# Experts of a two-block network: the gather and the return of tokens as single rounded products, weights of the slots beside the first expert, norms in one operation a block

## The reference, cut to what matters

```
hx2 = modulate(rmsnorm(x, norm2_g), mod_x[3], mod_x[4])     # x * rsqrt(mean x^2 + eps) * g * (1 + scale) + shift
probs = softmax(h @ router_w); sel = probs + router_b
best_group = argmax over 4 groups of the sum of the two best sel of its 4 experts
idx = the two best experts inside best_group; combine = their probs, normalised
for e in 16 experts: out += combine[:, e] * ((silu(h @ w_gate[e]) * (h @ w_up[e])) @ w_down[e])
x = x + mod_x[5] * out
return rmsnorm(x, final_norm_g)
```

## Time and profile before

| | |
|---|---|
| median of 3 runs | 1496.63 us (1496.12 to 1498.65) |
| the profiled execution | 1495.06 us |
| its span, first to last instruction | 1493.7 us |
| mean granted TensorE clock | 0.954 |
| PE busy | 1357.3 us (91%) |
| PEld busy | 1186.4 us (79%) |
| DVE busy | 1096.1 us (73%) |
| ACT busy | 751.1 us (50%) |
| HBM read | 309.49 MB |

### The profile page before, as it was taken

The page is one execution under the profiler, slowest core; times in us unless marked ns, Lnnn a source line. Parts: engine busy times, 40 slices in busy tenths (PEclk is TensorE's granted clock), DMA queues, the critical chain, the costliest instruction groups (busy, mean ns, idle before and its releaser), DMA issues.

```text
span 1493.7 us, 20983 instructions
## 1 busy us (share of the span) xinstructions
PE 1357.3 (91%) x7872; PEld 1186.4 (79%) x7872; DVE 1096.1 (73%) x1502; ACT 751.1 (50%) x956; POOL 0.4 (0%) x5
## 2 busy tenths in 40 slices
PE   6879799998999977999987899898699999999996
PEld 6778699997777766998986678898687787777884
DVE  5767678777697867686786757876566868788686
ACT  3432444453666674454433543443146757566563
POOL 0000000000000000000000000000000000000000
PEclk9969999999999988999999899999799999999999
DMA  8628686773677754756573252321075977878772
GB/s 332 231 104 312 196 309 247 279 277 144 214 277 268 262 190 155 289 208 215 184 252 115 92 183 71 100 71 40 1 239 174 349 250 274 279 240 325 240 258 104
DMA packets 84212, 311.90 MB, mean 209 GB/s; under 512 B 9488, under 2 KB 9712, under 8 KB 83504
## 3 DMA queue, kind: packets, MB, share of 16 engines
q1 hardware_dynamic: 82080, 298.88, 57.0%
q10 hardware_dynamic: 2032, 11.69, 2.4%
HBM read 309.49 MB, written 1.05 MB: 208 GB/s over the span
## 4 chain that ended last, share of the span: by engine, by line
PE 66%; DVE 22%; ACT 7%; DMA 3%; issue 2%; DVEq 0%; ACTq 0%; SPq 0%
PE ps L433 65%; DVE w_low L392 8%; DVE junk L392 4%; ACT w_high L392 3%; DMA ring<-stream 1%; DMA ring<-moe 1%; DVE t_one L392 1%; DVE r_two L392 1%; DVE rs L392 1%; DVE x L392 1%; ACT h_high L392 1%; DVE t_two L392 1%; PE ps L1032 1%; DVE y_experts L392 1%; DVE all L392 0%
## 5 line engine op out<-in xcount | busy, mean ns | idle before, releaser
L392 DVE TENSOR_TENSOR w_low<-ring,w_high 128x1024 fp32r<-128x1024 f32 x368 | 451.0, 1225 | 149.9 <-ACT w_high L392 120.0
L392 ACT ACTIVATE w_high<-ring 128x1024 fp32r<-128x1024 f32 x368 | 390.3, 1061 | 294.2 <-PE ps L433 173.6
L433 PE MATMUL ps<-x_high,w_high 128*128 128x256 f32 (+1 forms) x784 | 237.1, 302 | 34.4 <-DVE x_low L392 22.6
L433 PE MATMUL ps<-x_low,w_high 128*128 128x256 f32 (+1 forms) x784 | 233.9, 298 | 0.0
L433 PE MATMUL ps<-x_high,w_low 128*128 128x256 f32 (+1 forms) x784 | 233.7, 298 | 0.0
L433 PEld LDWEIGHTS ps<-x_high,w_high 128*128 128x128 f32 x784 | 155.5, 198 | 44.3 <-issue 16.1
L433 PEld LDWEIGHTS ps<-x_low,w_high 128*128 128x128 f32 x784 | 155.7, 199 | 2.5
L433 PEld LDWEIGHTS ps<-x_high,w_low 128*128 128x128 f32 x784 | 155.4, 198 | 2.8
L392 DVE CUSTOM_DVE_ANT_0 junk<-ring,cond 128x1024 f32<-128x1024 f32 x109 | 133.6, 1226 | 29.9 <-DMA ring<-stream 16.8
L433 PE MATMUL ps<-h_high,w_high 128*128 128x256 f32 x512 | 146.7, 287 | 6.6 <-DVE h_low L392 4.2
L433 PE MATMUL ps<-h_low,w_high 128*128 128x256 f32 x512 | 145.6, 284 | 0.0
(11 more groups left out here) (299 smaller groups left out, 2066.7 us busy)
## 6 DMA issues: line engine op xcount, KB each, us to landing
ring<-stream SPq DMA_DIRECT2D x376, 512.0 KB, 4.8
ring<-moe SPq DMA_DIRECT2D x192, 512.0 KB, 4.7
tab_two<-tab ACTq DMA_DIRECT2D x1, 2824.0 KB, 15.0
gw<-gw ACTq DMA_DIRECT2D x1, 2304.0 KB, 13.2
cond<-cvec ACTq DMA_DIRECT2D x3, 512.0 KB, 5.5
x<-xT ACTq DMA_DIRECT2D x1, 1024.0 KB, 11.7
ctx<-ctxT ACTq DMA_DIRECT2D x1, 1024.0 KB, 4.8
pos<-posT ACTq DMA_DIRECT2D x1, 1024.0 KB, 8.3
```

Source lines behind the costliest of these rows:

```text
L392: return op(*a, **k).then_inc(self.sem, 1)
L433: return pe.matmul(out, stationary, moving, start=start, stop=stop, skip_group_check=True)
```

## The change

- The tokens are held as a high and a low part. ACT writes the modulated T2 (bias added in ACT's Identity), so that DVE's norm is 8 operations on X with scale and root row in one. The transposes become plain products with the identity; after ACT's rounded copy (`XT[0]`) TensorE adds the product of minus identity and that copy to the same PSUM bank, and ACT copies what is left to `XT[1]`.
- ONEHOT and SCAT have type fp32r. Gather: a product of each part with ONEHOT into banks of its own, each one MATMUL instruction; ACT copies the high one, DVE the low one.
- The DIAG products go behind the first piece of gate(0), and the slots' weights behind gate(0).
- Results: ACT writes the rounded YS (two halves) or YES of group 0, DVE subtracts to get their low parts (`result_lows`), and the scatters are products of each part with SCAT. `summed` makes YES[0] after place 12, by two copies of 128x1024 once y_add is 10. The scatters wait for the low parts.
- The last norm is 8 operations with gain and root row in one.

The diff, cut to its core:

```diff
+Y_SUMS, Y_LOW = {4: 2, 8: 6, 12: 10}, {1: 4, 2: 8, 0: 12, 3: 14}
+XG_BANKS = ((4, 6), (5, 7), (2, 3), (4, 6))
...
tensor_program
-    pe.wait_ge(s.t2, 4 * MOD_MOE + 4)
-    for b in range(2):
-        for k in range(KT):
+    for k in range(KT):
+        if k % 2 == 0:
+            pe.wait_ge(s.x_high, x_splits(MOD_MOE) + k // 2 + 1)
+        for b in range(2):
             ins = mm(PS[:, 4 + b, 0:NE], m.T2[:, k, b * P:(b + 1) * P], m.par("rw", k * NE, NE), k == 0, k == KT - 1)
...
-            ins = pe.transpose(PS[:, 2 * b + k // 4, ...], m.T2[:, k, b * P:(b + 1) * P], m.ident)
+            ins = mm(PS[:, 2 * b + k // 4, ...], m.T2[:, k, b * P:(b + 1) * P], m.ident, k % 4 == 0, False)
+        ins.then_inc(s.xt_mm, 1)
+    for b in range(2):
+        pe.wait_ge(s.xt, b + 1)
+        for c in range(2):
+            ins = mm(PS[:, 2 * b + c, :], m.NEG, m.XT[0][:, b, c * 512:(c + 1) * 512], False, True)
...
+    def tokens(out, part, k, slots):
+        for b in range(2):
+            ins = mm(out, m.XT[part][:, b, k * P:(k + 1) * P], m.ONEHOT[:, b, slots], b == 0, b == 1)
+        return ins
+    pe.wait_ge(s.xt, 4)
     pe.wait_ge(s.onehot, 2)
+    for r in range(4):
+        if r == 3:
+            pe.wait_ge(s.xg_high, 1)
+            pe.wait_ge(s.xg_low, 1)
+        for part in range(2):
+            for j in range(2):
+                ins = tokens(PS[:, XG_BANKS[r][part], j * 256:(j + 1) * 256], part, 2 * r + j, slice(0, 256))
...
     def other_tokens():
         for k in range(KT):
+            pe.wait_ge(s.xg_high, 4 + max(k - 1, 0))
+            tokens(PS[:, 4 + k % 2, 0:CAP - 256], 0, k, slice(256, CAP)).then_inc(s.xg_mm, 1)
+            pe.wait_ge(s.xg_low, 4 + max(k - 1, 0))
+            tokens(PS[:, 6 + k % 2, 0:CAP - 256], 1, k, slice(256, CAP)).then_inc(s.xg_mm, 1)
...
     def scatter(i, r):
-        if i == 0:
-            pe.wait_ge(s.y_add, 6)
-        else:
-            pe.wait_ge(s.y_out, i + 2)
-            if i < 3:
-                pe.wait_ge(s.y_add, 2 * i)
+        pe.wait_ge(s.y_add, Y_LOW[i] - (i > 0 and r < 2))
...
-                mm(out, m.YE[:, 0, blk], m.SCAT[:, 0, :], True, False)
-                ins = mm(out, m.YE[:, 1, blk], m.SCAT[:, 1, :], False, True)
+                for n in range(4):
+                    ins = mm(out, m.YES[n % 2][:, n // 2, blk], m.SCAT[:, n // 2, :], n == 0, n == 3)
             else:
-                ins = mm(out, m.YS[:, blk], m.SCAT[:, i + 1, :], True, True)
+                for n in range(2):
+                    ins = mm(out, m.YS[n][:, blk], m.SCAT[:, i + 1, :], n == 0, n == 1)
...
scalar_program
+    for k in range(KT):
+        if k % 2 == 0:
+            act.wait_ge(s.t2, 4 * MOD_MOE + k // 2 + 1)
+        A(m.T2[:, k, :], m.T1[:, k, :], ACT.Identity, s.x_high if k % 2 else None, bias=m.MOD[:, 120 + k:121 + k])
...
     for p in range(NE):
         high_upto(w + 5)
+        if p > 0:
+            summed(p - 1)
         turned(p)
...
vector_program
-    rms_rows(9, m.X[:, :, :], m.T1[:, :, :])
-    modulate_norm(MOD_MOE, m.T1, "n2g", 120, 128)
+    op(vv.tensor_scalar, sc2, m.MOD[:, 128:136], 1.0, None, ALU.add)
+    op(vv.tensor_tensor, sc2, sc2, m.par("n2g", 0, 8), ALU.mult)
+    root(9)
+    for k in range(KT):
+        op(vv.scalar_tensor_tensor, m.T1[:, k, :], m.X[:, k, :], sc2[:, k:k + 1], m.RSTD, ALU.mult, ALU.mult, inc=...)
...
+    def result_lows(p):
+        i, j = EXPERTS[p]
+        if j == 3:
+            for c in range(2):
+                vv.wait_ge(s.y_out, {1: 4, 2: 6, 0: 8, 3: 10}[i] - 1 + c)
+                if i == 0:
+                    op(vv.tensor_tensor, m.YES[1][:, c, :], m.YE[:, c, :], m.YES[0][:, c, :].bitcast(F32), ALU.subtract, inc=s.y_add)
+                else:
+                    half = slice(c * 512, (c + 1) * 512)
+                    op(vv.tensor_tensor, m.YS[1][:, half], PS[:, 4 + c, :], m.YS[0][:, half].bitcast(F32), ALU.subtract, inc=s.y_add)
...
         low_upto(w + 4)
+        if p > 0:
+            result_lows(p - 1)
         if back is not None:
             results(back, 0)
...
-    rms_rows(10, m.X[:, :, :], m.T1[:, :, :])
+    root(10)
     for k in range(KT):
-        op(vv.tensor_scalar, m.X[:, k, :], m.T1[:, k, :], m.par("fing", k), None, ALU.mult, inc=s.final)
+        op(vv.scalar_tensor_tensor, m.X[:, k, :], m.X[:, k, :], m.par("fing", k), m.RSTD, ALU.mult, ALU.mult, inc=s.final)
```

More of the change, by code:

```diff
@@ L215, in __init__ @@
         self.KF = view("kf", aKF, 2048)
-        place(P)
+        self.NEG = rounded("neg_ident", place(P), P)
         aX, aXL = place(4096), place(4096)
@@ L314, in __init__ @@
         self.XGH, self.XGL = (rounded("xg_" + n, a, 8 * CAP).rearrange("p (k s) -> p k s", k=KT) for n, a in (("high", aX), ("low", aB)))
-        self.XT = view("x_tokens", aB + 5120, 2048).rearrange("p (b d) -> p b d", b=2)
-        self.ONEHOT = view("onehot", aB + 7168, 2 * CAP).rearrange("p (b s) -> p b s", b=2)
-        self.SCAT = view("scat", aB + 8448, 1280).rearrange("p (i t) -> p i t", i=5)
+        self.XT = tuple(rounded("x_tokens_" + n, a, 2048).rearrange("p (b d) -> p b d", b=2) for n, a in (("high", aB + 5120), ("low", aT1)))
+        self.ONEHOT = rounded("onehot", aB + 7168, 2 * CAP).rearrange("p (b s) -> p b s", b=2)
+        self.SCAT = rounded("scat", aB + 8448, 1280).rearrange("p (i t) -> p i t", i=5)
         self.ROUT = view("rout", aB + 9728, 1024)
@@ L323, in __init__ @@
         self.YE = view("y_experts", aKF, 2048).rearrange("p (a d) -> p a d", a=2)
-        self.YS = view("y_single", aT1 + 1024, 1024)
+        self.YES = tuple(rounded("y_experts_" + n, a, 2048).rearrange("p (a d) -> p a d", a=2) for n, a in (("high", aT2), ("low", aB + 5120)))
+        self.YS = tuple(rounded("y_single_" + n, a, 1024) for n, a in (("high", aT1 + 1024), ("low", aT1)))
     def place(self, n):
@@ L967, in tensor_program @@
     mm(PS[:, 6, 8:12], m.ONES, group_of(0), False, True).then_inc(s.cnt, 1)
-    pe.wait_ge(s.xt, 2)
-    pe.wait_ge(s.onehot, 2)
-    for k in range(KT):
-        for b in range(2):
-            ins = mm(PS[:, 4 + k // 2, (k % 2) * 256:(k % 2 + 1) * 256], m.XT[:, b, k * P:(k + 1) * P], m.ONEHOT[:, b, 0:256], b == 0, b == 1)
-        if k % 2:
-            ins.then_inc(s.xg_mm, 1)
-    pe.wait_ge(s.diag, 2)
-    for b in range(2):
-        ins = mm(PS[:, 2, b * P:(b + 1) * P], m.ONES, m.DIAG[:, b, :], True, True)
@@ L978, in tensor_program @@
-    ins.then_inc(s.db_mm, 1)
-    pe.wait_ge(s.comb_w, 1)
-    for i in range(5):
-        for b in range(2):
-            ins = mm(PS[:, 3, 4 * i:4 * i + 4], m.ONEHOT[:, b, i * P:(i + 1) * P], m.ROUT[:, 848 + 4 * b:852 + 4 * b], b == 0, b == 1)
-    ins.then_inc(s.cw_mm, 1)
+    def tokens(out, part, k, slots):
[3 more added lines that the diff above has]
+    pe.wait_ge(s.xt, 4)
+    pe.wait_ge(s.onehot, 2)
@@ L985, in other_tokens, with weights_of_slots @@
+    def weights_of_slots():
+        pe.wait_ge(s.comb_w, 1)
+        for i in range(5):
+            for b in range(2):
+                ins = mm(PS[:, 7, 4 * i:4 * i + 4], m.ONEHOT[:, b, i * P:(i + 1) * P].bitcast(F32), m.ROUT[:, 848 + 4 * b:852 + 4 * b], b == 0, b == 1)
+        ins.then_inc(s.cw_mm, 1)
     def other_tokens():
+        pe.wait_ge(s.scat, 5)
+        pe.wait_ge(s.cw, 1)
         for k in range(KT):
-            pe.wait_ge(s.xg_low, 4 if k < 4 else k + 1)
-            for b in range(2):
-                ins = mm(PS[:, 4 + k % 4, 0:CAP - 256], m.XT[:, b, k * P:(k + 1) * P], m.ONEHOT[:, b, 256:CAP], b == 0, b == 1)
@@ L1037, in down @@
         if j == 0 and i >= 2:
-            pe.wait_ge(s.y_out, i + 1)
+            pe.wait_ge(s.y_add, Y_LOW[i - 1])
         for n in range(4):
@@ L1479, in results, with summed @@
                 act.wait_ge(s.sc_mm, 4 * (i - 1))
-            A(m.YS, PS[:, 4:6, :].rearrange("p c n -> p (c n)"), ACT.Copy, s.y_out)
+            for c in range(2):
+                A(m.YS[0][:, c * 512:(c + 1) * 512], PS[:, 4 + c, :], ACT.Copy, s.y_out)
+    def summed(p):
+        if EXPERTS[p] == (0, 3):
+            act.wait_ge(s.y_add, Y_SUMS[p])
+            for a in range(2):
+                A(m.YES[0][:, a, :], m.YE[:, a, :], ACT.Copy, s.y_out)
     high_upto(W_MOE + 8)
@@ L2139, in vector_program, with first_low @@
         op(vv.tensor_scalar, m.DIAG[:, b, :], m.ident, dest[:, b:b + 1], None, ALU.mult, inc=s.diag)
+    def first_low(r):
+        vv.wait_ge(s.xg_mm, 2 * r + 2)
+        op(vv.tensor_copy, m.XGL[:, 2 * r:2 * r + 2, 0:256], PS[:, XG_BANKS[r][1], :].rearrange("p (k s) -> p k s", k=2), inc=s.xg_low)
+        low_upto(W_MOE + r + 1)
     first_max(ML, NE, EX, st[:, 34:36], TM)
     op(vv.scalar_tensor_tensor, ML, EX, -3e30, ML, ALU.mult, ALU.add)
+    for r in range(4):
+        first_low(r)
     first_max(ML, NE, E2, st[:, 36:38], TM)
```

52 lines of the change are left out of this document (33 added, 19 removed).

## The result

The changed kernel needs 1503.3 us (median of 6 runs, 1503.06 to 1504.44) beside 1496.72 us of the kernel before, measured with it. The ratio is 1.0039 with a 95% interval of 1.0026 to 1.0052, so it is slower by 0.26 to 0.52%. The profiled execution is 1503.29 us with a span of 1502.0.

What follows compares the result with a forecast made beforehand. TensorE bounds the experts, except where it stops. Front -0.8 - 3.3 - 1.35, group 1 +1.4 + 1.5, group 2 +0.8, group 0 +2.4 + 2.2, short stop +1.5, tail -1.7 make +2.65 us: 1497.7 profiled, 1499.3 median, range 1493.3 to 1504.

Steps and rivals of the forecast that it cites:

- Norm and router: From the MoE norm's reciprocal to the count: router ends 3.8 us sooner, transposes take most back, 0.8 us left.
- Gather: Gather of the tokens: 32 instructions in 5.7 us against 9.0 before, a gain of 3.3 us (2.0 to 5.0).
- Other slots: Other slots' products: 8.7 us against 10.0, with TensorE standing from +2.1 to +5.0; gain 1.35 us.
- one of two short stops: Half clock after the stops of 2.9 (other slots) and 2.4 us (group 2): one is paid, 1.5 us.
- Group 1: Return of group 1: TensorE stands 4.6 us; DVE's two extra operations cost +1.4 us, half clock 1.5 us.
- Group 2: Return of group 2: 2.4 us idle for the low part, less 1.6 given back by the products: +0.8 us.
- What follows is TensorE's: Behind group 2's return, with two tiles, TensorE sets the time; no size of its own.
- Group 0: Return of group 0: 5.8 us stop, less 4 x 0.93; taken as +2.4 us, plus 2.2 us of half clock.
- Tail: End of the kernel: new last norm -1.2 us, last square sums no longer queued -0.5; together -1.7 us.
- The clock holds: Rival: full clock through the new stops takes away 2.55 us, giving 1494.1 us; chance 0.18.
- The low parts come in time: Rival: the returns' 7.3 us are kept, 1482 us, believed only as far as 1489.6; chance 0.07.
- The slow rival: Rival: half clock for six us and more after every pause, +5.8 us on the sum, 1505 us; chance 0.17.

Runs made afterwards that it cites:

- norm_only: The kernel before with the new last norm and nothing else: 1495.04 us, ratio 0.9990.
- results_only: The kernel before with the split returns alone: 1510.64 us, ratio 1.0105.
- front_norm: The changed kernel with the plain returns put back: 1489.12 us, ratio 0.9954 of the kernel before.
- early_lows: The changed kernel with results' low parts made after gate(p+1)'s first low part, not its fourth, and ACT's group 0 copies two pieces earlier: 1493.86 us, ratio 0.9978.
- front_warm: front_norm with 14 unread products filling TensorE's stop among the other slots' products: 1487.36 us, ratio 0.9935.
- stops_warm: The changed kernel with unread products filling three stops (other slots, group 1, group 0): 1493.43 us, ratio 0.9983.
- warm_stop: The changed kernel with 24 unread products ahead of the wait of group 0's first scatter: 1500.19 us, ratio 1.0018.
- dve_extra: front_norm with unread DVE operations of like size added where the results' low parts would be made: 1493.8 us, ratio 0.9986.
- high_only: The changed kernel without the results' low parts: no subtraction, scatters of the high part alone: 1489.39 us, ratio 0.9961.

## Why the prediction was right or wrong

**Ahead of the change: not foreseen, +3.1 us.** The sum began at R9, with nothing ahead of it. R9 lies between 1056.89 and 1063.34 in the 14 profiles, and kernels alike up to there differ: norm_only and results_only, both of the old front, 1059.17 and 1056.89; front_norm and early_lows, both of the new one, 1060.06 and 1063.34. In the changed kernel two places are seen: the chain has a transfer of the stream of 5.28 us at 147.08 where the kernel before had 3.69 at 147.06, and 16 products at 155.73 that took 5.20 in place of 3.73 us, at half clock. All six runs of the changed kernel lie within 1.4 us, though. Nor is the slow form spread evenly over the 14 profiles: those 16 products took 3.72 us in the three kernels with the old front (before, results_only, norm_only) and in front_warm, and 5.1 to 6.7 us in the ten others, all with the new front; the mean of R9 is 1058.4 us with the old front and 1060.4 with the new one. So a part of the 3.1 us may belong to the changed program, although ahead of R9 it adds only two DVE operations on 8 columns. No run here isolates that, and it stays open.

**Norm and router: right.** The router starts 3.8 us nearer to R9, as worked out; the count gained 1.5 instead of 0.8, mostly as the router took 6.57 and not 7.0; the products with the identity took 5.9, as foreseen.

**Gather: right, a little slow.** 5.7 us foreseen, 6.4 measured up to the first product, since half clock lasted about 5.7 us in it, beside 4.1 us in the gather before. DIAG and weights gave nothing that shows.

**Other slots: right.** A stop of 2.9 us was foreseen, 2.47 + 0.37 came, with half clock behind it; front_warm prices that at 1.6 us, which was the sum's "one of two short stops" at 1.5. Front with this stop: -3.95 in the sum, -3.88 measured.

**Group 1: the mechanism right, the size too large.** The stop is 3.82 and not 4.6, T7 was 2.15 and not 2.9 us late, and 1.05 of it was back by T10: 1.1 in place of 2.9. The clock is priced at 1.4 by stops_warm (foreseen 1.5) and at 2.2 by warm_stop. DVE's work, foreseen as 1.4, is 0.7 in dve_extra, and high_only kept 0.6 of the 2.8 us that TensorE saves, where nothing was to be kept; both are within the spread of T5-T10, so how the 1.1 us divides is not shown.

**Group 2: the mechanism right, the delay too small.** The stop came as foreseen (2.57, foreseen 2.4) and the clock held, but the cost was 1.5 and not 0.8. The mis-sized term is the delay, 2.4. Counted from T10, the first scatter began after 17.26 us before (1354.41 to 1371.67) and after 20.27 us in the changed kernel (1354.36 to 1374.63): 3.0 us later, of which the trace counts 2.57 as idle. The low part came 0.5 us later after T10 than the prediction had it. On the way, at 1367.68, DVE waited 0.61 us for ACT's high part of a piece.

The products gave back what they should: 3.0 less the cost of 1.5 is 1.5, with 1.6 in the sum, though the sum's own terms, 0.45 + 3 x 0.45, make 1.8. "What follows is TensorE's" held too, since no stop of TensorE stands between this scatter and T12. In early_lows, by contrast, the same products brought nothing (48.66 beside 48.55), as there the wait had moved to DVE's `he`.

**Group 0: the stop to the digit, the cost too small.** 5.83 us beside 5.8; half clock 2.5 beside 2.2. But wait and work were 3.5 in place of 2.4. Counted from T12 the first scatter began 6.0 us later (28.77 us in place of 22.80), and warm_stop, with the same delay and no loss of clock, had 2.95 us of it back by T14 and 2.5 by T15, where 4 x 0.93 = 3.7 was taken as given back. So the term that was mis-sized is the saving of the products. What takes the rest is argued and not shown; DVE's two subtractions alone cost 1.9 us with nobody waiting (dve_extra), and early_lows, with a stop of 0.96 us, still loses 2.4.

**Tail: wrong, +0.9 in place of -1.7.** The norm gave its 1.2 us. The rest, foreseen as -0.5, was +2.1, with the clock at 0.57 from 1476 and at 0.63 from 1486. The prediction had no term for the clock here. The first of the two losses comes by stops that the kernel before has as well; the second comes behind the 0.78 us stop of the split return, which is the edit's. Without them the split return of group 3 goes the way that was said, by less: T15-R10 is 17.60 in early_lows and 17.84 in front_norm, 0.2 us.

**The rivals.** "The clock holds" is out: three of the stops lost it. "The low parts come in time" was false of the change and true of early_lows, and there its 7.3 us didn't come: TensorE's stops moved to DVE's `he` and low parts of weights. The slow rival gave a time nearest to the measured one, 1505, but for other reasons: only one of the two short stops was paid, the count came early and the gather took 6.4 and not 7.0 us; what made up the difference are the tail's clock and the stages ahead. By its section "HAM oscillation — how this bites in real kernels" the kernel on the Trainium skill's page "TensorE: Matmul & The Clock Gate", which the prediction names beside this rival, has waits of about 3 to 5 us. That the stops of 2.9 and 2.4 us would be paid as well doesn't follow from it; one of the two was.

**What it comes to.** The edits make +5.2 us of the 8.3: -4.3 up to T5, +1.1 for group 1, +1.5 for group 2, +6.0 for group 0, +0.9 for the tail. The sum had +2.65. About 1 us of the tail is the first loss of clock, which comes without the edit too, so without it the edits make about 4. That the range held the time is partly luck: 1503.3 lies above the forecast case's own range (1496.8 to 1501.8) and 0.7 us inside the upper bound, and 3.1 us of it come from stages that the sum left out. In the sum group 1 was 1.8 us too dear while group 2, group 0 and the tail were 0.7, 1.4 and 2.6 too cheap.

## What to carry to other kernels

Time that a faster product saves is only there if the engine that makes its operands has room: two subtractions of 1.3 us each cost 1.9 us in a place where nobody waited for them, and 2.8 us less of TensorE's work brought 2.2 us in one place and no more than 0.6 in another. Count a new wait from the milestone ahead of it to the first product behind it; the idle time in the trace can be less (2.57 us of idle time was a delay of 3.0). Ask of each new wait in a dense stretch what the idle time does to the clock as well; a stop of 5.8 us cost 2.5 us more behind it, and a filler of unread products takes that back if its length is priced from a row at full clock and ends inside the stop. When the change has independent halves, time them apart: here one gained 0.5% and the other more than took it.
